# Seven block products in place of eight for a third of the FFN down projection, with weight sums made by accumulating DMAs

## The reference, cut to what matters

```python
def swiglu(h, w1, w3, w2):
    return (jax.nn.silu(h @ w1) * (h @ w3)) @ w2

for l in range(DEPTH):
    h = rmsnorm(x, g_ffn1[l])
    x = x + 0.5 * swiglu(h, w1_a[l], w3_a[l], w2_a[l])
    ...                                   # the mixer
    h = rmsnorm(x, g_ffn2[l])
    x = x + 0.5 * swiglu(h, w1_b[l], w3_b[l], w2_b[l])
```

## Time and profile before

| | |
|---|---|
| median of the timed runs | 2257.19 us |
| span of the profiled execution | 2255.2 us |
| TensorE (matmul) busy | 2249.8 us, 11686 instructions |
| VectorE busy | 1546.0 us (69%) |
| ScalarE busy | 1238.9 us (55%) |
| weights' DMA queue | 415.76 MB, 53.3% of the 16 DMA engines |
| granted TensorE clock | 1.000 |

### The profile page before, as it was taken

How to read it: one execution, slowest core, us unless ns; L and a number is a source line. 1 busy time by engine, 2 the same in 40 slices (tenths; PEclk the granted TensorE clock), 3 DMA queues, 4 the chain that set the end, 5 groups by cost and what they waited for, 6 DMA issues and landing times.

```text
span 2255.2 us, 28960 instructions
## 1 busy us (share of the span) xinstructions
PE 2249.8 (100%) x11686; PEld 1920.7 (85%) x11686; DVE 1546.0 (69%) x2179; ACT 1238.9 (55%) x1489; POOL 0.2 (0%) x4
## 2 busy tenths in 40 slices
PE   9999999999999999999999999999999999999999
PEld 8888888888888888888888888888888888888887
DVE  7764567765774566775776599767657747976773
ACT  7644445554653544654554576465555537755652
POOL 0000000000000000000000000000000000000000
PEclk9999999999999999999999999999999999999999
DMA  7556455555555455554555553545555555345553
GB/s 264 205 198 219 168 191 175 196 196 174 191 187 205 168 175 199 187 197 169 201 190 202 192 169 129 206 155 191 206 177 187 185 180 195 109 172 196 184 191 126
DMA packets 176213, 417.61 MB, mean 185 GB/s; under 512 B 16816, under 2 KB 20784, under 8 KB 176080
## 3 DMA queue, kind: packets, MB, share of 16 engines
q1 hardware_dynamic: 175936, 415.76, 53.3%
q10 hardware_dynamic: 144, 0.00, 0.0%
HBM read 414.66 MB, written 1.05 MB: 184 GB/s over the span
## 4 chain that ended last, share of the span: by engine, by line
PE 98%; DMA 1%; DVE 0%; SPq 0%; ACT 0%; issue 0%; DVEq 0%
PE psum L666 25%; PE psum L602 17%; PE psum L604 17%; PE psum L603 17%; PE psum L667 13%; PE psum L677 3%; PE psum L634 2%; PE psum L685 2%; PE psum L976 1%; DMA xt_in<-t_xt_dram 0%; PE psum L797 0%; DMA raw<-t_gate_up_1a_dram 0%; PE psum L954 0%; PE psum L817 0%; PE psum L944 0%; PE psum L966 0%
## 5 line engine op out<-in xcount | busy, mean ns | idle before, releaser
L1646 DVE TENSOR_TENSOR split_w<-raw,split_w 128x2048 fp32r<-128x2048 f32 (+1 forms) x405 | 881.1, 2182 | 285.8 <-ACT split_w L1176 284.9
L1176 ACT ACTIVATE split_w<-raw 128x2048 fp32r<-128x2048 f32 (+1 forms) x405 | 736.2, 1828 | 311.1 <-PE psum L604 288.2
L666 PE MATMUL psum<-xt,split_w 128*128 128x512 f32 x2464 | 859.2, 393 | 0.1
L667 PE MATMUL psum<-xt,split_w 128*128 128x256 f32 x2464 | 689.2, 280 | 0.0
L666 PEld LDWEIGHTS psum<-xt,split_w 128*128 128x128 f32 x2464 | 461.2, 187 | 104.3 <-DVE split_w L1646 1.3
L667 PEld LDWEIGHTS psum<-xt,split_w 128*128 128x128 f32 x2464 | 465.3, 189 | 0.3
L602 PE MATMUL psum<-split_w,xt 128*128 128x512 f32 (+1 forms) x736 | 289.5, 393 | 0.0
L604 PE MATMUL psum<-split_w,xt 128*128 128x512 f32 (+1 forms) x736 | 283.7, 385 | 0.0
L603 PE MATMUL psum<-split_w,xt 128*128 128x512 f32 (+1 forms) x736 | 283.6, 385 | 0.0
L602 PE MATMUL psum<-split_w,ht_hi 128*128 128x512 f32 x700 | 272.9, 390 | 0.0
L604 PE MATMUL psum<-split_w,ht_lo 128*128 128x512 f32 x700 | 272.5, 389 | 0.0
(11 more groups left out here) (278 smaller groups left out, 1951.2 us busy)
## 6 DMA issues: line engine op xcount, KB each, us to landing
raw<-w_in_dram SPq DMA_DIRECT2D x180, 512.0 KB, 4.4
raw<-t_gate_up_1b_dram SPq DMA_DIRECT2D x88, 512.0 KB, 4.1
raw<-t_gate_up_2a_dram SPq DMA_DIRECT2D x88, 512.0 KB, 4.1
raw<-t_gate_up_2b_dram SPq DMA_DIRECT2D x88, 512.0 KB, 4.1
raw<-t_gate_up_1a_dram SPq DMA_DIRECT2D x84, 512.0 KB, 4.1
raw<-ffn_w_down_dram SPq DMA_DIRECT2D x80, 512.0 KB, 4.2
raw<-w_a_dram SPq DMA_DIRECT2D x40, 512.0 KB, 4.4
raw<-w_b_dram SPq DMA_DIRECT2D x40, 512.0 KB, 4.4
```

Source lines behind the costliest of these rows:

```text
L666: nc.tensor.matmul(bank, whi[:, slot, w], xt[:, c, :, :], start=c == 0, stop=False)
L667: last = nc.tensor.matmul(bank[:, 0:T], wlo[:, slot, w], xt_hi[:, c, :], start=False, stop=c == DC - 1)
L1176: nc.scalar.activation(whi[:, u % HL, 0:n], raw[:, r, 0:n], ACT.Copy).then_inc(hi_done, 1)
L1646: nc.vector.tensor_tensor(wlo[:, u % HL, 0:n], raw[:, r, 0:n], whi[:, u % HL, 0:n], ALU.subtract).then_inc(w_ready, 1)
```

## The change

Chunks 8 to 15 (`MIXED`) of each FFN's down projection are taken as a 2x2x2 block product: token halves by even and odd chunks by column halves. The four weight *quarters* are called 11, 21, 12, 22: first digit 1 for even chunks and 2 for odd ones, second digit the column half. Each quarter is 1 MB, as large as a unit. Seven products replace eight:

- the right operands 11, 21 and 22 are the quarters; U = 11 + 12, T2 = U + 22, T3 = 12 + 22 and T4 = T2 + 21 are sums. The signs are carried on the side of the activations and in the scale (`rhalf` or `minus_half`) with which a result is added to `x`;
- the sums are made by GpSimd with accumulating DMAs from SBUF to SBUF (`down_sums`), in place: 11 becomes U, then T2, then T4, and 12 becomes T3. Each waits until the operand that it overwrites has been split;
- the left operands for U, T3, T2 and 22 are four sums of activations (`sa`), made in the hidden stage by VectorE in blocks 9, 11, 13 and 15 from `hid` of that block and the one before, split like `ht`;
- the quarters do not pass through the three raw buffers: 11 and 21 are loaded after blocks 14's and 16's units, 12 and 22 into the memory of `xt`, once the last hidden block is through. Units of the raw ring are counted on their own (`place`);
- the results of 11 and T2 and T3 accumulate in one PSUM bank, which VectorE reads after 11, after T2 and after T3 (`taken` lets TensorE go on).

The order of the down stage is the table `DOWN`; its places are numbered 0 to 14. The other 14 chunks are computed as before.

The diff, cut to its core:

```diff
+QUARTERS = ("11", "21", "12", "22")
+MIXED = range(8, 16)
+DOWN = (("plain", 0, range(0, 4)), ("plain", 0, range(4, 8)), ("product", "11"), ("product", "21"),
+        ("plain", 0, range(16, 20)), ("product", "U"), ("product", "22"), ("plain", 1, range(0, 4)),
+        ("product", "T2"), ("plain", 0, range(20, 22)), ("product", "T4"), ("product", "T3"),
+        ("plain", 1, range(4, 8)), ("plain", 1, range(16, 20)), ("plain", 1, range(20, 22)))
+COMBINED = {"U": ("11", "12"), "T3": ("12", "22"), "T2": ("11", "22"), "T4": ("11", "21")}
+SPLIT_BEFORE = {"U": 2, "T3": 3, "T2": 5, "T4": 8}
+HALF_LAST = 11
...
-                r = e.unit(u) % RAW
-                eng.wait_ge(w_ready, units(e, u))
+                r = e.place(u) % RAW
+                eng.wait_ge(w_ready, RAW + RING_UNITS[e.place(u) - RAW] + 1)
...
+                    eng.dma_start(quarter[q][:, 1024 * j:1024 * j + 1024].rearrange("p (k n) -> p k n", k=2),
+                                  rows[:, 2 * j:2 * j + 2, row, 512 * col:512 * col + 512]
+                                  ).then_inc(quarter_in[q], 16)
...
+                    if b == 14:
+                        eng.wait_ge(ht_done, ffn_blocks(e, f, 2))
+                        quarter_load(w2, "11")
+                    if b == 16:
+                        quarter_load(w2, "21")
...
+                for i, part in enumerate(DOWN):
+                    if i == 12:
+                        eng.wait_ge(w_used, units(e, u0 + 2 * FG - 1, HL))
+                        quarter_load(w2, "12")
+                        quarter_load(w2, "22")
+                    if part[0] == "plain":
+                        _, half, chunks = part
+                        plain(w2, FF, P * chunks[0], 512 * half, u0 + 2 * FG + i, len(chunks))
...
+                LEFT = {"11": lambda i: token_half(HT, first[i], 0), "21": lambda i: token_half(HT, second[i], 0),
+                        "T4": lambda i: token_half(HT, second[i], 1), "U": lambda i: summed(i, 0),
+                        "T3": lambda i: summed(i, 1), "T2": lambda i: summed(i, 2), "22": lambda i: summed(i, 3)}
+                EACH, BOTH = pair(0, 0), pair(0, 1)
+                OUT = {"11": (EACH, True, True), "T2": (EACH, False, True), "T3": (EACH, False, True),
+                       "U": (BOTH, True, True), "21": (pair(2, 0), False, False), "T4": (pair(2, 1), False, True),
+                       "22": (pair(1, 0), True, False)}
...
+                    eng.wait_ge(w_ready, units(e, u, RAW))
+                    for i in range(4):
+                        hi, lo = LEFT[name](i)
+                        w = slice(i * 512, (i + 1) * 512)
+                        nc.tensor.matmul(out, hi, whi[:, slot, w], start=start and i == 0, stop=False,
+                                         skip_group_check=resumed)
+                        nc.tensor.matmul(out, hi, wlo[:, slot, w], start=False, stop=False, skip_group_check=resumed)
+                        last = nc.tensor.matmul(out, lo, whi[:, slot, w], start=False, stop=stop and i == 3,
+                                                skip_group_check=resumed)
+                    last.then_inc(w_used, 1)
...
-                for i in range(5):
-                    blocks(u + i, 0, 2, HT, range(4 * i, 4 * i + 4), i == 0, False, True)
+                blocks(u, 0, 2, HT, range(0, 4), True, False, True)
+                blocks(u + 1, 0, 2, HT, range(4, 8), False, False, True)
+                eng.wait_ge(pair_free, ffn_blocks(e, f, FC - 1))
+                product(u + 2, "11")
+                product(u + 3, "21")
+                blocks(u + 4, 0, 2, HT, range(16, 20), False, False, True)
+                product(u + 5, "U")
+                product(u + 6, "22")
+                blocks(u + 7, 0, 1, HT, range(0, 4), (False, True), False, True)
+                eng.wait_ge(taken, 2 * ffns(e, f) + 1)
+                product(u + 8, "T2")
                 eng.wait_ge(ht_done, ffn_blocks(e, f, FC - 1))
-                blocks(u + 5, 0, 2, HT, (20, 21), False, True, True)
-
-                u += 6
-                blocks(u, 0, 1, HT, (0, 1), True, False, False)
+                blocks(u + 9, 0, 2, HT, (20, 21), False, (True, False), True)
+                product(u + 10, "T4")
+                eng.wait_ge(taken, 2 * ffns(e, f) + 2)
+                product(u + 11, "T3")
+
+                u += 12
+                blocks(u, 0, 1, HT, (4, 5), False, False, False)
                 if next_stage != "end":
                     eng.wait_ge(done, e.after(done, ("x", next_stage, 0)))
                     x_transposes(next_stage, 0)
...
+                blocks(u, 2, 1, HT, (6, 7), False, False, True)
...
+                def sums_rounded(i):
+
+                    eng.wait_ge(sums_done, 4 * ffns(e, f) + i + 1)
+                    nc.scalar.activation(sa_hi[:, i, :, :], sa[:, :, :], ACT.Copy).then_inc(sums_hi, 1)
...
-                    split(u0 + b + 4)
...
+                    if b in second:
+                        sums_rounded(second.index(b))
+                    if b + 4 < 2 * FG:
+                        split(u0 + b + 4)
+                    else:
+                        down_split(b + 4 - 2 * FG)
...
+                for name, (into, other) in COMBINED.items():
+                    eng.wait_ge(w_ready, units(e, u0 + 2 * FG + SPLIT_BEFORE[name], RAW))
+                    for q in (into, other):
+                        eng.wait_ge(quarter_in[q], 32 * (ffns(e, f) + 1))
+                    if name in ("T3", "T2"):
+                        eng.wait_ge(combined["U"], 16 * (ffns(e, f) + 1))
+                    if name == "T4":
+                        eng.wait_ge(combined["T2"], 16 * (ffns(e, f) + 1))
+                    eng.dma_start(quarter[into], quarter[other], accum_op=ALU.add).then_inc(combined[name], 16)
...
+                    both = hid.rearrange("p two (m t) -> p two m t", m=MT)
+                    e.link(nc.vector.tensor_tensor(sa[:, 0, :], both[:, 0, 1, :], both[:, 1, 1, :], ALU.subtract))
+                    nc.vector.tensor_tensor(sa[:, 1, :], both[:, 0, 0, :], both[:, 0, 1, :], ALU.subtract)
+                    e.link(nc.vector.tensor_tensor(sa[:, 2, :], sa[:, 0, :], both[:, 0, 0, :], ALU.subtract))
+                    nc.vector.tensor_tensor(sa[:, 3, :], sa[:, 2, :], both[:, 1, 0, :], ALU.add).then_inc(sums_done, 1)
...
-                    split(u0 + b + 3)
+                    if b + 3 < 2 * FG:
+                        split(u0 + b + 3)
+                    else:
+                        down_split(b + 3 - 2 * FG)
+                    if b in second:
+                        eng.wait_ge(hid_done, ffn_blocks(e, f, b))
+                        sums()
...
+                    if b in second:
+                        sums_lo(second.index(b))
+                down_split(3)
+                EACH, BOTH = psum[:, 0, :], psum[:, 1, :]
+                down_split(4)
+                down_split(5)
+                multiplied(u0 + 2 * FG + 2)
+                part_to_x(0, 0, EACH, rhalf).then_inc(taken, 1)
+                down_split(6)
+                down_split(7)
+                down_split(8)
+                down_split(9)
+                down_split(10)
+                multiplied(u0 + 2 * FG + 5)
+                for m in range(MT):
+                    part_to_x(m, 1, BOTH, rhalf)
+                down_split(11)
+                split_before(11)
+                multiplied(u0 + 2 * FG + 8)
+                part_to_x(0, 1, EACH, minus_half).then_inc(taken, 1)
+                down_split(12)
+                down_split(13)
+                split_before(12)
+                multiplied(u0 + 2 * FG + 10)
+                e.link(add_to_x(2, 0, hidden=True))
+                multiplied(u0 + 2 * FG + 11)
+                last = part_to_x(1, 0, EACH, rhalf)
+                if next_stage == "end":
+                    last.then_inc(out_ready, MT)
+                else:
+                    last.then_inc(done, e.mark(done, ("x", next_stage, 0)))
+                e.link(part_to_x(1, 1, EACH, minus_half))
...
```

More of the change, by code:

```diff
@@ L451, in wide, with quarter_load, ffn_loads @@
                     plain(w, D, 4 * P * k, col, u + k, 4, cols)
-            def ffn_loads(u0, gate_up_w, w2):
+            def quarter_load(w2, q):
+                first = e.lay * FF + P * MIXED.start
+                rows = w2[first:first + P * len(MIXED), :].rearrange("(k two p) n -> p k two n", two=2, p=P)
+                row, col = int(q[0]) - 1, int(q[1]) - 1
+                for j in range(2):
+                    eng.dma_start(quarter[q][:, 1024 * j:1024 * j + 1024].rearrange("p (k n) -> p k n", k=2),
+                                  rows[:, 2 * j:2 * j + 2, row, 512 * col:512 * col + 512]
+                                  ).then_inc(quarter_in[q], 16)
+            def ffn_loads(u0, f, gate_up_w, w2):
                 w2 = flat(w2)
@@ L591, in blocks @@
                 hi, lo = split
-                slot = u % HL
+                slot = e.unit(u) % HL
```

(4 more changed lines are left out.)

163 lines of the change are left out of this document (116 added, 47 removed).

## The result

The changed kernel takes 2383.97 us (median of four runs, 2378.67 to 2388.25) against 2257.28 on the same chip: ratio 1.056, 95% interval 1.0546 to 1.0574. That is 127 us slower; the forecast was 44 slower. The profiled execution spans 2376.8 us, 121.6 more than before.

A forecast was written before the change was run, and what follows sets the result against it. TensorE's unbroken row of matmuls was taken as the bound. Per FFN, -2.7 (fewer matmuls) + 2.1 (hidden stage) + 6.1 (late accumulation chain) = +5.5 us; times 8, +44 on 2257 gives 2301 us, range 2240 to 2400.

The forecast's parts named there:

- T0: Start of the down stage in any FFN, from which the forecast counts the times of its chain.
- S: Down stage: time a 1 MB accumulation keeps the 16 DMA engines, taken as 5.2 us, bounds 3.0 and 9.1.
- D: Down stage: an accumulation's time from issue to landing, S + 1.5, taken as 6.7 us.
- Rival 2: Down stage: weight loads beside the sums contend for DMA engines, 7.5 us more per FFN, 2361 us; chance 0.20.
- U lands at 8.0 + D: Down stage, first sum: quarter 12 has landed 8.0 us after the stage's start, and U lands one accumulation later.
- a sign of being wrong: Transposes in place 12: TensorE was to idle there, 6.1 us per FFN; no idle would mean the forecast is wrong.
- Rival 3: TensorE's clock falls in chain waits, the next 12 matmuls run at 1.2 GHz: 22 us more, 2323; chance 0.10.
- The hidden stage, +2.1: Hidden stage: rounding the sums before ScalarE's split makes TensorE wait 2.1 us by block 19 in each FFN.
- T0 - 0.8 before, + 3.1: Start of down stage: VectorE's split of place 1 frees the raw buffer at 2.3, with 3.1 us lateness from block 20.
- The gain, -21.8: Down stages: 12 fewer matmuls in each of 8 FFNs, 96 in all, save 21.8 us.
- the loads are the same bytes: Weight loads: the change loads the same bytes as before; no cost was forecast for it.
- Break-even at D = 5.3: Down stage: the change neither gains nor loses if an accumulation lands in 5.3 us, where the lateness is 0.6 us.

The follow-up runs named there:

- e3: The changed kernel with the activation sums rounded one block later, behind ScalarE's `low` and VectorE's `ht_lo`; GpSimd's DMAs stay: 2342.65 us, ratio 1.0374.
- e5: The changed kernel with GpSimd's four DMAs per FFN copying the second quarter over the first and adding nothing: 2296.05 us, ratio 1.0177.
- e10: The changed kernel with the loads of the units at places 12 to 14 of `DOWN` cut to 64 KB each: 2355.65 us, ratio 1.0432.
- e4: The changed kernel with 8 unused matmuls before product T2 and 24 before T4, to keep TensorE busy: 2380.82 us, ratio 1.0544.
- e6: The changed kernel without the load of quarter 22, with 21 standing in for it everywhere: 2379.48 us, ratio 1.0538.
- e11: e7 with the spacer 32 bytes narrower, so that `ht_hi` and all behind it stand at their old addresses: 2236.48 us, ratio 0.991.
- e7: The changed kernel with VectorE making the weight sums and the activation sums rounded one block later: 2251.41 us, ratio 0.9975.
- e9: The kernel before the change with only an unused two-column tensor added ahead of the spacer: 2275.5 us, ratio 1.0079.
- e12: The changed kernel with the spacer 32 bytes narrower and nothing else: 2376.92 us, ratio 1.0534.
- e2: The changed kernel with the four weight sums made by VectorE in place of GpSimd's DMAs: 2265.27 us, ratio 1.0033.
- run 397: Not a run label: the text says that float32r matmuls of 128x512 run 397 ns a row, in place of 390.

## Why the prediction was wrong

The direction, the place and the order of the chain were right; the sizes of its links were not. The steps, in the mean of eight FFNs, by GpSimd's issues behind T0:

| | forecast | measured | e3 | e5 | e10 |
|---|---|---|---|---|---|
| U issued, behind T0 | 8.0 | 10.4 | 8.3 | 10.6 | 10.6 |
| U's issue to T3's | 6.7 | 9.6 | 8.8 | 6.1 | 7.7 |
| T3's issue to T2's | 4.1 | 4.0 | 4.0 | 4.0 | 4.0 |
| T2's issue to T4's | 11.9 | 14.2 | 14.3 | 9.8 | 13.7 |
| T4 to landing | 6.7 | 8.4 | 8.5 | 5.6 | 7.6 |
| T4 landed, behind T0 | 37.4 | 46.6 | 43.8 | 36.0 | 43.6 |
| T4 landed to the stage's end | 26.8 | 27.3 | 27.2 | 27.1 | 27.3 |

(The forecast column is its formulas at S = 5.2 and D = 6.7; T2's to T4's is D + S - 4.1, and 4.1 for the split; the last row is its 14.9 to the transposes and 58.05 - 46.2 behind them.)

The last row is the same within 0.2 us in all these runs, and in e4 (27.1), at clocks from 0.979 to 1.000: the landing of T4 sets the end of the down stage, and behind it the working holds to 0.5 us. What failed stands ahead of it. Put the measured landing of T4 into the forecast's own sum and it nearly comes out: 46.6 is 9.2 later, 8 x (-2.7 + 2.1 + 6.1 + 9.2) = +118 where +127 was measured; for e5, 1.4 earlier, it gives 8 x 4.1 = +33 where +39 was.

- **S and D, the term that failed.** The landing of a sum, D = S + 1.5 = 6.7, was worked out for an idle machine, and three of the four sums run beside the stream. U, T2 and T4 landed in 9.0, 9.5 and 8.4 us, where the forecast has 6.7, 7.8 (D + S - 4.1, behind T3) and 6.7: 5.7 of the 9.2 us. Of these 5.7, e10 gives back 3.2 by taking the stream away; 2.5 are left without it, so D was short by itself too (T3 takes 7.2). Engine time was sized right: S is 5.7 beside the stream and 7.1% x 2354.3 / 32 = 5.2 in e10, forecast 5.2. Rival 2 had the mechanism, but with 22's load in it, which e6 acquits, and 7.5 us a stage; e10's time gives 3.5 (28.3 / 8). It should have been in the forecast and not beside it, since the earlier trace rows showed 66% of the engines taken.
- **"U lands at 8.0 + D".** Off by 2.4 at the issue. The release was forecast at T0 + 2.3 and was at T0 + 1.4 in the third FFN (4.0 in the first). The landing of 12 was the error: I took 4.4 us from the earlier trace rows for its second half, which goes out behind the unit's two DMAs and its own first half, and it took 6.6 (6.5 in e6, without 22's two behind it). A further 0.6 us at each link, from landing to GpSimd's issue, had no term.
- **Where TensorE waits.** The forecast compared the chain's end with the transposes only. The same working has T4's split through at 41.5, where TensorE is at 38.1: 3.4 of the 6.1 would have fallen at T4. Measured, T4's product starts at T0 + 49.4 in the third FFN; 6.90 us fall there and 2.40 at T2, and next to nothing at the transposes (0.6 us in the whole program), which the forecast had named as a sign of being wrong. The half clock behind T4 hides the rest of VectorE's adds, which e4 uncovers.
- **Rival 3, the clock.** The trace shows it: behind 15 of the 16 waits at T2 and T4, 6 to 13 rows are 0.36 to 0.43 us apart in place of 0.23, 149 in all, or 28 us. The mechanism was right and its 22 us near, and the Trainium skill's rule ("TensorE: Matmul & The Clock Gate", "What's actually happening") names it. But I added it to the end's lateness, and e4 gets nothing back that can be told from none (3 us, with overlapping intervals): slow matmuls in the shadow of another engine are free.
- **The hidden stage, +2.1.** TensorE waits 1.31 us, and the stage is 1.7 longer. The lateness left behind it, 3.1 in the release "T0 - 0.8 before, + 3.1", delays 12's load by 2.1 us (the changed kernel against e3). Forecast, the two are 5.2 us a stage, or 42; e3 prices both at 41. Some of that is luck: both were too large, by 0.4 and 1.0 a stage, and of the 2.8 us that e3 takes off a down stage 0.8 are U landing sooner.
- **The gain, -21.8.** e11 gets 20.6 (2257.1 - 2236.5), so the count was right. The changed kernel did not have it to give: "the loads are the same bytes" was followed by no look at what the new tensors do to the addresses of the old. 32 bytes cost 15 us (e7 against e11), 18 in the kernel before (e9), and 7 or less in the changed one (e12).
- **Break-even at D = 5.3.** With 27.3 us behind T4's landing and 1.7 lost in the hidden stage, a down stage breaks even when T4 lands at 60.77 - 1.7 - 27.3 = 31.8, and the forecast's D = 5.3 puts it just there (12.1 + 3 x 5.3 + 3.8). e5's copies land in 4.8 to 5.6 us and T4 landed at T0 + 36.0 all the same, since U's issue was late and each link has its 0.6; it is D that the break-even was worked out in, and the landing of T4 that decides.

The sum of the parts, each step a pair of runs and the steps in this order: -20.6 (e11), +14.9 for the address (e7), +13.9 for the early rounding without DMAs (e2), and +118.7 for moving the four sums from VectorE to GpSimd's DMAs (the changed kernel), together +127. Of the last, 88 is the addition (e5), and the other 31 the DMAs' chain itself. In another order the shares differ: with the DMAs in place the rounding is worth 41 and the address 7 or less.

The Trainium skill's "Collectives: The Full Stack", "The bandwidth ceiling", has a reduce in the DMA engine at about half a copy's rate; the ratio of 1.87 agrees.

**Why U is slow in some FFNs.** From U's issue to T3's it is 12.5 us in the second FFN, where the others have 8.9 to 10.4. What differs is which DMA is issued first, U or the stream's unit at place 12. In the second FFN SP issues that unit 0.27 us ahead of U, in the third 0.84 behind it. Of the 4.74 us that follow U's issue, the DMA queues' lines are, in the second FFN (GpSimd's queue, q0, has none) and then in the third:

```profile
q1 hardware_dynamic: 559, 1.09, 88.7%
```

```profile
q0 software_dynamic: 80, 0.66, 72.0%
```

In the changed kernel, e3, e4, e12 and e6 (which lacks 22's load alone) there are 40 such U's. In 11 the unit's first half is issued ahead of U or at most 0.44 us behind it, and U lands in 9.7 to 11.9 us; in 29 it is 0.50 or more behind, and U lands in 8.0 to 8.7. No run sets that order on purpose, so it stands as what goes together and not as a cause.

What stays open: how a 32-byte shift slows the read of an operand (only the addresses 130688 and 130720, and what follows them, were tried); and whether the 7 us of e12 are real. Splitting the sums in two DMAs, so that the first half can be split sooner, was not tried, nor holding SP's unit back until U has landed.

## What to carry to other kernels

A sum that sits in a chain of landing, splitting and summing again belongs on the engine that splits, if that has room: on VectorE one took 2.28 us and hid (busy for 49.2 of 58.05 us in e11), where a DMA took 7.2 to 9.5 in the mean and 0.6 from landing to the next issue. When a forecast multiplies one unknown landing by four, take the landing with the traffic that will really be beside it, give each link the time from landing to the next issue, and follow a lateness across the stage's end until an engine is idle again. And when tensors are added, look where the matmul's operands come to stand, and time the kernel before with the same shift.

## What the hardware showed that I had not expected

- An SBUF-to-SBUF accumulation of 1 MB lands in 7.0 to 7.8 us with no unit of the stream beside it (T3), and in 8.0 to 9.3 beside one (U and T4), but in 9.7 to 11.9 where the unit was issued first or hardly later (U). A copy of the same size lands in 4.4 to 6.5. In engine time they are 5.7 us, 5.2 with the stream's short loads (e10), and 3.1.
- float32r matmuls of 128x512 run 397 ns a row in place of 390 (0.70 us for three in place of 0.68) when their `ht` operands stand 32 bytes off a multiple of 128.
- TensorE's clock can fall after the wait, in the middle of a full row of matmuls. Of the eight waits at T2, those of 2.61, 2.82 and 4.70 us were followed by half clock from the first row, and those of 1.87, 2.43, 2.70 and 2.77 by two to five rows at full pace and then half clock; only behind the one of 2.40 did it stay whole. The fifth FFN's, behind 1.87 us of idling, with the granted clock third from the end:

```profile
1300.31:1301.60 1.29, 1.29 (x6) 1.06 (x7) 1.29 (x2) 1.22 (x1) 0.89 (x1) 1.00 0.99 203
1301.60:1304.00 2.40, 2.40 (x7) 1.92 (x6) 2.40 (x2) 0.00 (x0) 0.00 (x0) 0.50 1.10 218
```
